# MLP of a decoder step: stored sums of w_up's blocks, and another beginning of a chunk's last w_down group

## The reference

```python
x = x + rmsnorm(merge(h_a, oa, y_b, y_c, g_mlstm, w_out, x.dtype), g_post_mix)
u = jax.nn.relu(jnp.einsum('btd,df->btf', rmsnorm(x, g_pre_mlp), w_up))
x = x + rmsnorm(jnp.einsum('btf,fd->btd', jnp.square(u), w_down), g_post_mlp)
```

## Time and profile before

| | us |
|---|---|
| median of 3 runs (lowest, highest) | 3834.09 (3819.32, 3837.29) |
| the profiled execution's own time | 3839.2 |
| its span | 3837.6 |
| TensorE matmul busy in the span | 3464.3 (90%) |
| DVE busy | 2049.5 (53%) |
| ACT busy | 1561.5 (41%) |
| GpSimd busy | 737.3 (19%) |

### The profile page before, as it was taken

The page is one execution under the profiler, slowest core; times in us unless marked ns, Lnnn a source line. Parts: engine busy times, 40 slices in busy tenths (PEclk is TensorE's granted clock), DMA queues, the critical chain, the costliest instruction groups (busy, mean ns, idle before and its releaser), DMA issues. The chain is left out here.

```text
span 3837.6 us, 61229 instructions
## 1 busy us (share of the span) xinstructions
PE 3464.3 (90%) x21989; PEld 2976.2 (78%) x21989; DVE 2049.5 (53%) x4128; ACT 1561.5 (41%) x3047; POOL 737.3 (19%) x1044
## 2 busy tenths in 40 slices
PE   8999999899958896678997995999989999999996
PEld 8999999444436664545665784999989999899996
DVE  2211100589946555744665446565675656756564
ACT  3321111688823433322444224444455434554342
POOL 0111100467712334422442001000010000200000
PEclk9999999899958786688999997999999999999998
DMA  6564443210054316576996553434444344432222
GB/s 206 204 208 153 155 148 125 86 42 9 9 124 87 80 34 166 153 207 206 358 355 210 168 175 116 139 123 138 139 141 157 116 153 135 139 108 67 69 75 77
DMA packets 444516, 533.48 MB, mean 139 GB/s; under 512 B 94885, under 2 KB 382246, under 8 KB 439238
## 3 DMA queue, kind: packets, MB, share of 16 engines
q1 hardware_dynamic: 415584, 410.59, 35.0%
q0 software_dynamic: 20992, 66.08, 5.2%
q10 hardware_dynamic: 7656, 53.04, 4.1%
HBM read 435.82 MB, written 143.91 MB: 151 GB/s over the span
## 5 line engine op out<-in xcount | busy, mean ns | idle before, releaser
L3453 PE MATMUL p_DP<-p_UH,p_WH 128*128 128x352 f32 x1536 | 497.6, 324 | 21.2 <-issue 14.4
L3454 PE MATMUL p_DP<-p_UL,p_WH 128*128 128x352 f32 x1536 | 496.6, 323 | 0.0
L3455 PE MATMUL p_DP<-p_UH,p_WL 128*128 128x352 f32 x1536 | 496.3, 323 | 0.0
L3453 PE MATMUL p_UP<-p_TH,p_WH 128*128 128x352 f32 x1344 | 438.8, 327 | 53.8 <-DVE p_TL L3363 36.9
L3454 PE MATMUL p_UP<-p_TL,p_WH 128*128 128x352 f32 x1344 | 433.6, 323 | 0.0
L3455 PE MATMUL p_UP<-p_TH,p_WL 128*128 128x352 f32 x1344 | 433.6, 323 | 0.0
L408 PE MATMUL p_PP<-p_WH,p_HH 128*128 128x384 f32 (+1 forms) x1224 | 416.6, 340 | 8.4 <-DVE p_HL L342 4.4
L409 PE MATMUL p_PP<-p_WL,p_HH 128*128 128x384 f32 (+1 forms) x1224 | 407.0, 332 | 0.0
L410 PE MATMUL p_PP<-p_WH,p_HL 128*128 128x384 f32 (+1 forms) x1224 | 406.7, 332 | 0.0
L3453 PEld LDWEIGHTS p_DP<-p_UH,p_WH 128*128 128x128 f32 x1536 | 290.7, 189 | 23.4 <-issue 21.3
L321 ACT ACTIVATE p_PT<-p_PP,p_rs 128x384 f32<-128x384 f32 (+1 forms) x153 | 87.3, 571 | 530.1 <-PE p_PP L410 530.1
(11 more groups left out here) (454 smaller groups left out, 6833.4 us busy)
## 6 DMA issues: line engine op xcount, KB each, us to landing
p_WU<-in_w_up SPq DMA_DIRECT2D x48, 1024.0 KB, 5.4
p_WD<-in_w_down SPq DMA_DIRECT2D x192, 256.0 KB, 2.9
cw_K<-in_cache_sb_k SPq DMA_DIRECT2D x192, 192.0 KB, 4.2
cw_V<-in_cache_sb_v POOLq DMA_DIRECT2D x192, 192.0 KB, 5.1
out_s_wk<-in_cache_win_k ACTq DMA_DIRECT2D x64, 382.5 KB, 3.5
out_s_wv<-in_cache_win_v ACTq DMA_DIRECT2D x64, 382.5 KB, 4.1
p_HH<-scratch_xh SPq DMA_DIRECT2D x34, 512.0 KB, 4.6
p_HL<-scratch_xl SPq DMA_DIRECT2D x34, 512.0 KB, 5.3
```

What stands on the lines that cost most here:

```text
L3453: pe.matmul(out, hi, rhi, start=first, stop=False, skip_group_check=True)
L3454: pe.matmul(out, hi, rlo, start=False, stop=False, skip_group_check=True)
L3455: return pe.matmul(out, lo, rhi, start=False, stop=last, skip_group_check=True)
```

## The change

The change has three parts, all in `mlp_phase`.

1. DVE makes the sums S1 to S4 in chunk 0 only. There, SP stores the four sums of each pair, 1 MB, to the DRAM array `su` once the last is made (`keep_sums`), and DVE makes a pair's sums only when the store of the pair before has landed. In chunks 1 and 2 SP loads them: S1 to S3 (768 KB) once the block S1 of the pair before has been split, S4 (256 KB) once its block S4 has (`load_sums`).
2. In a chunk's last w_down group, TensorE first makes, for both halves of tiles 0 and 1, the products with pair 14 (24 matmuls), waits for pair 15, and then makes the products with pair 15. Four PSUM banks are open in the meantime.
3. ACT does the hidden quarter 3 of the pair before ahead of the weight block, in every segment, and DVE the quarters 2 and 3 at the start of w_down groups.

```diff
@@ weight_ready
+            elif LHS[i][0] == "S" and c == 0:
+                eng.wait_ge(sc_ok, 4 * pair(c, x) + SUMS.index(LHS[i]) + 1)
             elif LHS[i][0] == "S":
-                eng.wait_ge(sc_ok, 4 * pair(c, x) + SUMS.index(LHS[i]) + 1)
+                eng.wait_ge(s4_in if LHS[i] == "S4" else s_in, 16 * (pair(c, x) - PAIRS + 1))
@@ SP
-                    sp.wait_ge(sc_ok, 4 * (u - 1))
+                    sp.wait_ge(sc_ok, 4 * min(u - 1, PAIRS))
...
+            def keep_sums(p):
+                sp.wait_ge(sc_ok, 4 * p + 4)
+                sp.dma_start(S["su"][p], SC[:, :, :, :].rearrange("p s k n -> p (s k n)")).then_inc(su_out, 16)
+
+            def load_sums(c, p, last):
+                u = pair(c, p)
+                if u == PAIRS:
+                    sp.wait_ge(su_out, 16 * PAIRS)
+                sp.wait_ge(wl_ok, block(*divmod(u - 1, PAIRS), "S4" if last else "S1") + 1)
+                a, e = (3, 4) if last else (0, 3)
+                sp.dma_start(SC[:, a:e, :, :].rearrange("p s k n -> p (s k n)"), S["su"][p, :, a * 512:e * 512]).then_inc(s4_in if last else s_in, 16)
...
+                        if c == 0 and x == 0 and i == 0:
+                            keep_sums(0)
+                        if c == 0 and x + 1 < PAIRS and i == 5:
+                            keep_sums(x + 1)
+                        if PAIRS <= pair(c, x) + 1 < NCH * PAIRS and i in (1, 4):
+                            load_sums(*divmod(pair(c, x) + 1, PAIRS), i == 4)
                         if i == 6 and pair(c, x) + 2 < NCH * PAIRS:
                             up(pair(c, x) + 2)
@@ ACT
-                    high(w + AHEAD)
                     if i == 0 and before:
                         hidden(*before, 3)
                         before = None
+                    high(w + AHEAD)
@@ DVE, sums
                     if u:
                         dve.wait_ge(wl_ok, block(*divmod(u - 1, PAIRS), name) + 1)
+                        dve.wait_ge(su_out, 16 * u)
@@ DVE
+                    if kind == "D" and i == 0 and before:
+                        hidden(*before, 2)
+                        hidden(*before, 3)
+                        before = None
                     low(w + AHEAD)
...
-                        if i in (2, 3, 4) and pair(c, x) + 1 < NCH * PAIRS:
-                            sums(*divmod(pair(c, x) + 1, PAIRS), (SUMS[:2], SUMS[2:3], SUMS[3:])[i - 2])
+                        if c == 0 and i in (2, 3, 4) and x + 1 < PAIRS:
+                            sums(c, x + 1, (SUMS[:2], SUMS[2:3], SUMS[3:])[i - 2])
@@ TensorE (part: the matmuls of some of a tile's four blocks; bank_free: the wait for its PSUM bank)
             def down(c, g, j):
                 w = number["D", c, g, j]
+                if g == NG - 1 and j < 2:
+                    if j:
+                        return
+                    pe.wait_ge(ul_ok, 4 * pair(c, GRP * g + 1))
+                    for k in range(2):
+                        pe.wait_ge(wl_ok, w + k + 1)
+                        for n in range(2):
+                            bank_free(c, g, k, n)
+                            part(c, g, k, n, (0, 1))
+                    pe.wait_ge(ul_ok, 4 * pair(c, GRP * g + 1) + 4)
+                    for k in range(2):
+                        for n in range(2):
+                            part(c, g, k, n, (2, 3)).then_inc(mm_ok if n else dn_ok, 1)
+                    return
```

More of the change, by code:

```diff
@@ L3016, in mlp_phase @@
         sc_ok = m.sem("sc_ok")
+        su_out = m.sem("su_out")
+        s_in = m.sem("s_in")
+        s4_in = m.sem("s4_in")
         wh_ok = m.sem("wh_ok")
@@ L3479, in up, with part, bank_free @@
                 ins.then_inc(mm_ok, 1)
+            def part(c, g, j, n, fs):
+                w, i = number["D", c, g, j], ((c * NG + g) * KD + j) * 2 + n
+                cols = slice(n * H, (n + 1) * H)
+                for f in fs:
+                    s = pair(c, GRP * g + f // 2) % 3
+                    ins = product(down_bank(i), WH[w % RW][:, f, :], WL[w % RW][:, f, :], UH[s][:, f % 2, cols], UL[s][:, f % 2, cols],
+                                  f == 0, f == 3)
+                return ins
+            def bank_free(c, g, j, n):
+                i = ((c * NG + g) * KD + j) * 2 + n
+                if i >= 4:
+                    summed(pe, i - 4)
+                if c and g == 0 and i % (2 * KD) == 0:
+                    pe.wait_ge(zn_ok, c * TQ)
             def down(c, g, j):
                 w = number["D", c, g, j]
+                if g == NG - 1 and j < 2:
[12 more added lines that the diff above has]
+                    return
                 pe.wait_ge(wl_ok, w + 1)
@@ L3486, in down @@
                 for n in range(2):
-                    i = ((c * NG + g) * KD + j) * 2 + n
-                    if i >= 4:
-                        summed(pe, i - 4)
-                    if c and g == 0 and i % (2 * KD) == 0:
-                        pe.wait_ge(zn_ok, c * TQ)
-                    for f in range(4):
-                        s = pair(c, GRP * g + f // 2) % 3
-                        cols = slice(n * H, (n + 1) * H)
-                        ins = product(down_bank(i), WH[w % RW][:, f, :], WL[w % RW][:, f, :], UH[s][:, f % 2, cols], UL[s][:, f % 2, cols],
-                                      f == 0, f == 3)
-                    ins.then_inc(mm_ok if n else dn_ok, 1)
+                    bank_free(c, g, j, n)
+                    part(c, g, j, n, range(4)).then_inc(mm_ok if n else dn_ok, 1)
             def turn(c, q):
@@ L3533, in build @@
         ("x1", (TP, D)),
-        ("hT", (KD, P, TP)))}
+        ("hT", (KD, P, TP)),
+        ("su", (KF // 2, P, 4 * 512)))}
     project_phase(nc, A, S, O)
```

## The result

The change took 3854.7 us (median of 6 runs, 3847.2 to 3857.8), the kernel before 3825.8 us (6 runs, 3819.3 to 3837.3). The ratio is 1.0071, with a 95% interval of 1.0058 to 1.0084: slower by 0.7%, some 27 us. The time is not the forecast's, 3838, but the second rival's, 3855, and lies inside the stated range. Both were built on 3834.1 us, the median of the three runs of before that were known; over six runs it is 3825.8. So the measured difference is 27 to 29 us (by the ratio and by the medians), where the forecast had +4 and the second rival +21. By the prediction's own line of 0.5% the change is slower, the outcome that had a chance of 0.16, and not "no change", which had 0.74.

What follows compares the result with a forecast made beforehand. TensorE's matmul pace bounds the kernel, with DVE under cover, so only waits at the passages could be won. The terms, -14.6 - 5.4 + 23 + 1 = +4 us, on a median of 3834.1 gave 3838 us, range 3815 to 3858.

Steps and rivals of the forecast that it cites:

- second rival: Chunk 0, third tile of groups 0 to 6: every wait brings the half clock; +21 us, 3855 us; chance 0.18.
- term 1: Each chunk's last w_down group: starting with the ready pair fills the wait; -14.6 us, 7.2 of it in chunk 2.
- term 2: Passages to chunks 1 and 2: without sums on DVE, waits shrink by 2.7 us each; -5.4 us.
- (4): Sign to look for: the passages' other TensorE waits shrink by 2 to 3 us each.
- term 3: Chunk 0: storing sums from SP's queue delays w_down's blocks, about 3 us a group, 6 in group 4; +23 us.
- term 4: Smaller edits: hidden work before weight copies costs where slack is short, loads of sums hide; +1 us.
- first rival: Chunk 0: the store of the sums is not felt, costing 3 us; -16 us, 3818 us; chance 0.19.
- the third (stored sums too late): Chunks 1 and 2: stored sums arrive late, trading DVE work for DMA waits; 3860 us and more; chance 0.03.

Runs made afterwards that it cites:

- run 7: run 4 with hidden work ahead of the weight block kept for the last w_down group alone; 3819.4 us, 0.9990 of the kernel before.
- Run 11: run 10 with the sums made on DVE in every chunk, nothing stored or loaded; 3825.0 us, 0.9993 of the kernel before.
- run 10: run 9's GpSimd token transfers, plus DVE's additions before its tokens in the first three tiles of chunks 0 and 1's last group; 3823.5 us, 0.9994 of before.
- run 3: The change with sums made on DVE everywhere, nothing stored or loaded, but SP still held in chunk 0 for the last sum; 3836.8 us, 1.0025 of before.
- run 4: The change with chunk 0's store moved behind the w_up load, or behind a w_down group's first w_down load; 3819.0 us, 0.9983 of before.
- run 12: run 10 with DVE's additions before the tokens in seven of the last group's eight tiles; 3827.9 us, 1.0005 of before.
- run 9: run 4 with the next chunk's third- and fourth-quarter token transfers issued by GpSimd instead of SP; 3819.7 us, 0.9981 of before.

## Why the prediction was right or wrong

**The last group (term 1): half right.** The two facts that it was built on were measured as foretold: the wait before the group falls to 0.22 us with no half clock behind it, three times, and the third tile waits 2.85 us in chunks 0 and 1 and not at all in chunk 2. Chunk 2 gave 7.18 us for 7.2. But the step "So 3.7 us are won" in chunks 0 and 1 counted until the third tile and stopped there. A wait for w_down's block and one for the tokens, further on, took it all back, +0.4 us in each. The term was -6.3 us, not -14.6. The clue stood in the row that I used: if DVE empties the bank behind the token work, the token work is what bounds the passage, and TensorE has only moved to another place in its queue.

**The passages (term 2): right, a bit smaller.** They lose 2.7 and 1.5 us less, where 2.7 each were foretold: -4.2 for -5.4. DVE's combination went from 6.4 us to 1.5 in what TensorE waits for, as (4) had it. But the sums are not all of it. The waits for ACT's emptying of a bank, 5.2 us in the rows of before, have left the passages as well, and that is mostly the new order's work, which the term did not name: in run 7, with the old order there, 3.5 us of them stand again. Against that, the waits for a weight block's low part grew from 12.0 us in the MLP to 16.1. Run 11 against run 10 gives the sums 3.0 us in both passages.

**The store in chunk 0 (term 3): the waits are right to a microsecond, the price of a wait is not.** The seven waits come to 23.3 us from start to start, for 23, with group 4 at 5.6 for 6 and the five others at 2.2 to 3.6 for 3.0. The change over run 3 (26.7 us for the store, with SP held alike) and run 4 (gone, with the store behind the block) show that the cause is the one named, the block's place behind the store. The term had that with the hold and the w_up load in one sum; the hold has 5.0 us of it. What failed is the step that left the half clock to a rival, on the ground that "one of 2.47 us at 2865.15 let the next matmul run in 0.40 us". All six groups from group 1 on have a stretch of half clock, also behind 2.21 us, and the loss behind the waits is 10.5 us. The rival had priced it at 13. The row at 2865.15 could not carry it: in this kernel's traces the same wait stands with and without a half clock behind it.

**The smaller edits (term 4): +1 foretold, +2.4 found.** 1.2 us at the start of chunk 0, where slack is short, and 1.2 us in group 4 of chunk 1, where the loads of the stored sums stand in the queue with the token loads and ACT waits 2.7 us for a w_down block. There the step "The loads of sums in chunks 1 and 2 hide" was too quick: no wait for a stored sum shows, but they have a price for another load in that one place.

**The sum.** 4 foretold; to it come term 3's 10.4 (33.4 for 23, nearly all of it the 10.5 us behind the waits), term 1's 8.3, term 2's 1.2, term 4's 1.4, and 0.4 at the end: 25.7, what the lost time without the ramp gives. Every term had its sign, and the first rival (the store is not felt) and the third (stored sums too late) fell. The second rival's mechanism is half of the miss; the other half is the last group's give-back, which no rival had. That its 3855 meets the measured 3854.7 is luck: it is +21 on a time of before that was 8.3 us higher than the six runs' median, and counted from that median it would be 3847. The range held the time by the same luck: as a difference it ended at +24.

## What to carry to other kernels

A transfer that nobody waits for still costs if it stands ahead of one that somebody does, and still more if its queue is held for it: look at what is issued within some microseconds behind it, and issue it one place later before you take it out. A gain at a wait is only worth what is left when the same engine's next waits are read as well; when the releaser of the next one stands behind a stream of other work, that stream is the bound and the gain will reappear further down. And where waits of two to six microseconds on TensorE repeat, the half clock behind them belongs in the sum (here 1.4 to 2.6 us each), not in a rival.

## What the runs showed of the hardware that I had not expected

- A wait of one length does and does not bring the half clock. In the change's trace a wait of 2.21 us is followed by granted clock 0.50 and one of 2.85 us by 1.00. Across the runs the same wait of 2.9 us before the third tile of the last group (lost 3.09) has nothing behind it in the change and 1.55 us in run 4.
- The half clock behind the shorter waits does not begin with the first matmul: in group 1 five run at full rate and the sixth is at 0.49 us; behind 5.63 us the first already takes 0.63.
- A store of one megabyte issued right behind a block left it nearly as early as no store at all when it stood in the same queue (2.4 us lost in seven groups against 2.1), and cost 4 us in the one group with token loads ahead when it stood in another queue (6.2 us).

What stays open: run 12's MLP is as short in its profile as run 9's (1459.1 us), and yet its median is 8 us higher (ratios 1.0005 and 0.9981, intervals apart). Run 12's profiled execution took 3820.2 us, 7.8 us less than its median, so its profile is not that of a typical one, and it can't tell whether the 8 us are in the MLP or ahead of it. The same holds for the 5 us of run 3 that its MLP does not show. Nor does any run have the store ahead of the block in another queue.
